# A transformer step of 1072 tokens: chunks of 384, 384 and 304, two long blocks, and a new order at the norms

## The chip, the core and the metric

The kernel runs on one core of a Trainium2 chip (trn2). The metric is the device time of one execution in microseconds; the median of several runs is what counts.

## What is computed

One step of a one-layer encoder for 1072 tokens (16 meta tokens, 1024 of a prompt, 32 of running streams), width 1024, in float32:

```python
def swiglu(x, wg, wu, wd):
    return (jax.nn.silu(x @ wg) * (x @ wu)) @ wd
def ffn_step(h, g, b, wg, wu, wd):
    return layer_norm(ALPHA * h + 0.5 * swiglu(h, wg, wu, wd), g, b)
```

A first such step (hidden width 2816) with norm ln1; then one product with `w_in` that gives the inputs of two mixers, a sparse attention whose keys are picked by an index score, and a recurrence; then `mixer_output`, in which each mixer's output goes through a projection, is weighted by a gate, and the sum through `w_out`, with norm ln2; then a second feed-forward step with norm ln3.

## The kernel before, in words

Activations lie transposed in SBUF: `c.y` holds 128 rows of the width on the partitions, 8 slices of them, by 1072 tokens. Every large product is exact to nearly float32 by splitting both operands into a high and a low part: `product3` (line 63) issues three products (L65 to L67) into one bank of PSUM. ScalarE makes the high parts, GpSimd or VectorE the low ones (the "rests").

Tokens are taken in the chunks of line 31, `[(0, 358), (358, 358), (716, 356)]`; tiles of 128 tokens (`TT`) are used where tokens are turned to or from the partitions.

`build` (line 1849) runs seven phases, each a block of its own that ends with `end_phase` (clear the semaphores, a barrier over all engines):

- `load_inputs` (line 110): SyncE loads tiles of tokens into three buffers, TensorE transposes each (L152), ScalarE makes `h_hi` and `y` (L169, L170), VectorE `h_lo` (L177). The first weights of ffn1 are loaded ahead (L133).
- `ffn` (line 295) for ffn1: 11 groups of 256 hidden rows, of two tiles j. An "up" is one (j, chunk): 48 products for gate and up, then silu on ScalarE (L373), the product and its split on VectorE (L485, L490, L492). Then the "downs": 8 outputs of 6 products per chunk into two banks, which VectorE adds to `y` (L504). The first group is ordered by chunk, all others by tile; all six ups come ahead of the three downs. GpSimd makes the weights' rests (L418, L425).
- `index_and_project` (line 730): first norm ln1 (class `Norm`, line 181). Per chunk: `mean` (L215) and `variance` (L224) are products with a matrix of ones on TensorE, `centre` is on VectorE (L274), `squares` (L240) and `deviation` (L247) on ScalarE, `scale_shift` on VectorE (L281 reciprocal, L287 two multiplications, L291 eight scale-and-shifts, then the rest of the second half, L262); `heads` (L252) makes `h_hi` on ScalarE, the first half's rest is GpSimd's. All three chunks' means and variances are issued together; then tiles 0 and 1 of the projection (class `Projection`, line 654) go chunk by chunk, every later tile by itself. ScalarE drains, `QueryStack` splits the index queries (L637, L643), and the index scores follow (L650, L651).
- `mixers` (line 1139).
- `mixer_output` (line 1682): four pairs of tiles t. Per pair all six ups (24 products each, L65 to L67 into `mo_psa` and `mo_psb`), the gated sum on VectorE (`mix`), then the downs of three chunks into four banks, which VectorE adds to `y` (L1842, L1846). `y` comes back from DRAM during the second tile (L1725).
- `ffn` for ffn2 with ln2 at its head, and `last_norm` (line 514): nine tiles are transposed back (L555), VectorE makes the moments (L592 to L601), ScalarE normalises (L582), GpSimd multiplies by gamma (L566), VectorE adds beta (L611), SyncE stores.

Every engine runs its list of instructions in order and waits on semaphores; the order of each list is written by hand.

Of the kernel before, what the change touches and what calls it, by code (L numbers as in the profile page):

```python
# [7 lines left out]

# [22 lines left out]
CHUNKS = [(0, 358), (358, 358), (716, 356)]  # L31
# [37 lines left out]

class Core:  # L70


# [13 lines left out]
    def sb(self, stack, name, shape, dtype=F32):  # L86
        return stack.enter_context(self.nc.sbuf_tensor(name, shape, dtype))

    def ps(self, stack, name, shape):
        return stack.enter_context(self.nc.psum_tensor(name, shape, F32))  # L90

# [18 lines left out]
def load_inputs(c, dram):  # L110

    nc = c.nc
    with ExitStack() as st:
        x = c.sb(st, "ld_x", [P, 3, D])
        psT = [c.ps(st, f"ld_ps{i}", [P, KD * P]) for i in range(2)]
        x_in = [c.sem(f"ld_x_in{i}") for i in range(3)]
        ident_ready, w_in = c.sem("ld_ident"), c.sem("ld_w")
        turned, hi_done, lo_done, y_done = (c.sem("ld_" + n) for n in ("turned", "hi", "lo", "y"))
        n_dma = [sum(bool(token_rows(t, *r)) for r in ((0, N_META), (N_META, LP), (LP, T))) for t in range(len(TT))]
        with nc.Block() as block:  # L120
            @block.sync
            def _(sp):
                for t in range(len(TT)):
                    if t >= 3:
                        sp.wait_ge(turned, t - 2)
                    for src, r0, r1 in ((dram["meta"], 0, N_META), (dram["x_prompt"], N_META, LP),
                                        (dram["x_sample"], LP, T)):
                        if (rows := token_rows(t, r0, r1)):
                            p0, n, at = rows
                            sp.dma_start(x[p0:p0 + n, t % 3, :], src[at:at + n, :]).then_inc(x_in[t % 3], 16)  # L130
                    if t == 4:
                        for i, part in enumerate(("ffn1_wg", "ffn1_wu")):
                            sp.dma_start(c.up_raw[:, i], dram[part].rearrange("(k p) m -> p k m", p=P)[:, :, 0:2 * P]).then_inc(w_in, 16)  # L133
                sp.wait_ge(w_in, 32)

            @block.gpsimd
            def _(pool):
                pool.memset(c.ident[:], 0.0).then_inc(ident_ready, 1)
                pool.wait_ge(ident_ready, 1)
                pool.affine_select(out=c.ident[:], in_=c.ident[:], compare_op=ALU.not_equal, fill=1.0, base=0,  # L140
                                   pattern=[[-1, P]], channel_multiplier=1).then_inc(ident_ready, 1)

            @block.tensor
            def _(pe):
                pe.wait_ge(ident_ready, 2)
                for t, (t0, n) in enumerate(TT):
                    pe.wait_ge(x_in[t % 3], 16 * sum(n_dma[t % 3:t + 1:3]))
                    if t >= 2:
                        pe.wait_ge(lo_done, t - 1)
                        pe.wait_ge(y_done, t - 1)  # L150
                    for k in range(KD):
                        last = pe.transpose(psT[t % 2][:, k * P:k * P + n], x[0:n, t % 3, k * P:(k + 1) * P],  # L152
                                            c.ident[0:n, 0:n])
                    last.then_inc(turned, 1)

            drain_transposed(c, block, psT, turned, hi_done, lo_done, y_done)


def transposed(ps, n):
    return ps[:].rearrange("p (k t) -> p k t", k=KD)[:, :, 0:n]  # L160


def drain_transposed(c, block, psT, turned, hi_done, lo_done, y_done):

    @block.scalar
    def _(act):
        for t, (t0, n) in enumerate(TT):
            act.wait_ge(turned, t + 1)
# [12 lines left out]
class Norm:
# [4 lines left out]
    def __init__(self, c, st, name, banks, eps, scratch=None):  # L186
        self.c, self.name, self.banks, self.eps_value = c, name, banks, eps
        sb = lambda n, s: c.sb(st, f"{name}_{n}", s)
        self.gamma, self.beta, self.eps, self.ones = sb("gamma", [P, KD]), sb("beta", [P, KD]), sb("eps", [P, 1]), sb("ones", [P, P])
        self.sd, self.rstd = sb("sd", [P, 358]), sb("rstd", [P, 358])  # L190
        self.sq = sb("sq", [P, 2, 2, 358]) if scratch is None else scratch
# [103 lines left out]
def ffn(c, dram, name, norm_name=None):  # L295

    nc = c.nc  # L300
    wg = dram[name + "_wg"].rearrange("(k p) m -> p k m", p=P)
    wu = dram[name + "_wu"].rearrange("(k p) m -> p k m", p=P)
    wd = dram[name + "_wd"].rearrange("(n p) m -> p n m", p=P)
    with ExitStack() as st:
        sb = lambda n, s, d=F32: c.sb(st, f"{name}_{n}", s, d)
        sem = lambda n: c.sem(f"{name}_{n}")

        up_raw = sb("up_raw", [P, 2, KD, 2 * P]) if norm_name else c.up_raw
        loads_ahead = 0 if norm_name else 1
        up_hi = sb("up_hi", [P, 2, 2, KD, P], F32R)  # L310
        up_lo = sb("up_lo", [P, 2, 2, KD, P], F32R)
        dn_raw = sb("dn_raw", [P, 2, D])
        dn_hi = sb("dn_hi", [P, 2, D], F32R)
        dn_lo = sb("dn_lo", [P, 2, D], F32R)
        hid_hi = sb("hid_hi", [P, 2, T], F32R)
        hid_lo = sb("hid_lo", [P, 2, T], F32R)
        gate = sb("gate", [P, 2, 358])
        prod = sb("prod", [P, 2, 358])
        ps_gate = [c.ps(st, f"{name}_psg{i}", [P, 512]) for i in range(3)]
        ps_up = [c.ps(st, f"{name}_psu{i}", [P, 512]) for i in range(3)]  # L320
        ps_dn = [c.ps(st, f"{name}_psd{i}", [P, 512]) for i in range(2)]
        up_in, dn_in = sem("up_in"), sem("dn_in")
        up_hi_done, up_lo_done, dn_hi_done, dn_lo_done = sem("uphi"), sem("uplo"), sem("dnhi"), sem("dnlo")
        up_mm, dn_mm = sem("up_mm"), sem("dn_mm")
# [1598 lines left out]
```

## Time and profile before

| | us |
|---|---|
| runs, median (lowest to highest of 3) | 2971.89 (2968.1 to 2976.58) |
| span of the profiled execution | 2966.0 |
| load to the first feed-forward product | 0 to 40.40 |
| ffn1 | 40.40 to 829.1 |
| ln1, first projection tiles, to the first score | 829.1 to 961 |
| scores, selection, rest of the projection | 961 to 1465 |
| mixers | 1465 to 1880 |
| mixer_output | 1880 to 2082.7 |
| ln2 and ffn2 | 2082.7 to 2921.6 |
| last norm | 2921.6 to 2966 |

The page gives no time of the profiled execution besides its span, the time from its first to its last instruction; the runs contain what lies around it. Engines are named PE (TensorE), PEld (its weight loads), DVE (VectorE), ACT (ScalarE), POOL (GpSimd), SP (SyncE). PEclk is the mean clock that TensorE was granted, 1.00 being 2.4 GHz. A matmul's own duration overlaps that of the next, so starts tell the spacing.

### The profile page before, as it was taken

The numbers are of one execution on the slowest core, as the hardware profiler recorded it, in microseconds if no ns is written. First come the engines' busy times: TensorE is split into PE (matmuls) and PEld (weight loads), VectorE is DVE, ScalarE is ACT, GpSimd is POOL, SyncE is SP. The second block draws the span as 40 slices with busy tenths as digits, with TensorE's granted clock in tenths as the row PEclk, the third lists the DMA queues.
The fourth block names the chain that finished last, engine by engine and source line by source line (L and its number), as shares of the span: only waits on it lengthen the run. The fifth ranks groups of instructions, "written<-read, shape, count | busy, mean of one in ns | idle before, by whom it ended". The sixth has DMA issues, their size and how long they took to land. (4 is left out here: it accounts for less than half of the span.)

```text
span 2966.0 us, 41425 instructions
## 1 busy us (share of the span) xinstructions
PE 2739.8 (92%) x16384; PEld 2638.8 (89%) x16384; DVE 1378.5 (46%) x2882; ACT 632.2 (21%) x1081; POOL 513.7 (17%) x183
## 2 busy tenths in 40 slices
PE   6999999999978999999869986799799999999995
PEld 6999999999957899999759975799599999999995
DVE  1333333333356689993075526666553333333336
ACT  3111111111023622122245533210311111111102
POOL 1211111122012012112100002121221112222112
PEclk9999999999988999999858987799999999999997
DMA  3111111111022011222200000422211111111101
GB/s 130 53 48 42 42 42 42 42 42 42 1 60 63 22 36 43 95 88 95 89 15 31 1 1 8 154 67 73 71 43 43 42 42 42 42 50 49 42 0 73
DMA packets 134941, 149.13 MB, mean 50 GB/s; under 512 B 19072, under 2 KB 119520, under 8 KB 134704
## 3 DMA queue, kind: packets, MB, share of 16 engines
q1 hardware_dynamic: 131376, 134.45, 14.4%
q10 hardware_dynamic: 3456, 13.17, 1.1%
q8 instruction: 75, 1.23, 0.2%
q14 instruction: 34, 0.28, 0.0%
HBM read 123.82 MB, written 23.79 MB: 50 GB/s over the span
## 5 line engine op out<-in xcount | busy, mean ns | idle before, releaser
L485 DVE TENSOR_TENSOR ffn_prod<-ffn_gate,ffn_psu 128x358 f32<-128x358 f32 x132 | 69.6, 527 | 808.3 <-ACT ffn_gate L373 808.3
L65 PE MATMUL ffn_psg<-h_hi,ffn_up_hi 128*128 128x358 f32 (+1 forms) x1056 | 345.4, 327 | 23.8 <-DVE h_lo L262 12.5
L65 PE MATMUL ixp_ps<-h_hi,ixp_hi 128*128 128x358 f32 (+1 forms) x1032 | 338.7, 328 | 24.3 <-issue 17.3
L65 PE MATMUL ffn_psd<-ffn_hid_hi,ffn_dn_hi 128*128 128x358 f32 (+1 forms) x1056 | 346.6, 328 | 11.4 <-DVE y L504 10.4
L504 DVE TENSOR_TENSOR y<-y,ffn_psd 128x358 f32<-128x358 f32 (+1 forms) x480 | 251.0, 526 | 209.4 <-PE ffn_psd L67 209.4
L66 PE MATMUL ffn_psg<-h_lo,ffn_up_hi 128*128 128x358 f32 (+1 forms) x1056 | 346.1, 328 | 0.0
L67 PE MATMUL ffn_psg<-h_hi,ffn_up_lo 128*128 128x358 f32 (+1 forms) x1056 | 345.5, 327 | 0.0
L373 ACT ACTIVATE ffn_gate<-ffn_psg 128x358 f32<-128x358 f32 x132 | 62.0, 470 | 1329.7 <-PE ffn_psu L67 1329.7
L66 PE MATMUL ffn_psd<-ffn_hid_lo,ffn_dn_hi 128*128 128x358 f32 (+1 forms) x1056 | 344.5, 326 | 0.0
L66 PE MATMUL ffn_psu<-h_lo,ffn_up_hi 128*128 128x358 f32 (+1 forms) x1056 | 344.3, 326 | 0.0
L67 PE MATMUL ffn_psd<-ffn_hid_hi,ffn_dn_lo 128*128 128x358 f32 (+1 forms) x1056 | 344.3, 326 | 0.0
L67 PE MATMUL ffn_psu<-h_hi,ffn_up_lo 128*128 128x358 f32 (+1 forms) x1056 | 343.6, 325 | 0.0
L65 PE MATMUL ffn_psu<-h_hi,ffn_up_hi 128*128 128x358 f32 (+1 forms) x1056 | 342.6, 324 | 0.0
L66 PE MATMUL ixp_ps<-h_lo,ixp_hi 128*128 128x358 f32 (+1 forms) x1032 | 338.9, 328 | 0.0
L67 PE MATMUL ixp_ps<-h_hi,ixp_lo 128*128 128x358 f32 (+1 forms) x1032 | 337.6, 327 | 0.0
L425 POOL TENSOR_TENSOR ffn_dn_lo<-ffn_dn_raw,ffn_dn_hi 128x2048 fp32r<-128x2048 f32 x22 | 101.8, 4626 | 892.3 <-ACT ffn_dn_hi L379 892.3
L65 PEld LDWEIGHTS ffn_psg<-h_hi,ffn_up_hi 128*128 128x128 f32 x1056 | 200.0, 189 | 25.1 <-issue 14.8
L65 PEld LDWEIGHTS ffn_psd<-ffn_hid_hi,ffn_dn_hi 128*128 128x128 f32 x1056 | 198.0, 188 | 26.3 <-DVE y L504 16.4
L65 PEld LDWEIGHTS ixp_ps<-h_hi,ixp_hi 128*128 128x128 f32 x1032 | 195.9, 190 | 26.0 <-issue 21.8
L67 PEld LDWEIGHTS ffn_psg<-h_hi,ffn_up_lo 128*128 128x128 f32 x1056 | 200.2, 190 | 0.0
L66 PEld LDWEIGHTS ffn_psg<-h_lo,ffn_up_hi 128*128 128x128 f32 x1056 | 199.9, 189 | 0.0
L66 PEld LDWEIGHTS ffn_psd<-ffn_hid_lo,ffn_dn_hi 128*128 128x128 f32 x1056 | 199.1, 189 | 0.0
(289 smaller groups left out, 4936.2 us busy)
## 6 DMA issues: line engine op xcount, KB each, us to landing
ffn_dn_raw<-in_ffn_wd SPq DMA_DIRECT2D x22, 1024.0 KB, 4.9
ixp_raw<-in_w_in SPq DMA_DIRECT2D x39, 512.0 KB, 3.8
spill<-y ACTq DMA_DIRECT2D x24, 536.0 KB, 2.7
up_raw<-in_ffn_wg SPq DMA_DIRECT2D x11, 1024.0 KB, 5.4
up_raw<-in_ffn_wu SPq DMA_DIRECT2D x11, 1024.0 KB, 7.9
ffn_up_raw<-in_ffn_wg SPq DMA_DIRECT2D x11, 1024.0 KB, 5.4
ffn_up_raw<-in_ffn_wu SPq DMA_DIRECT2D x11, 1024.0 KB, 7.9
mo_sig<-spill SPq DMA_DIRECT2D x16, 536.0 KB, 4.7
```

Of the source, the lines that this page charges most:

```text
L65: pe.matmul(out, w_hi, x_hi, start=first, stop=False)
L66: pe.matmul(out, w_hi, x_lo, start=False, stop=False)
L67: return pe.matmul(out, w_lo, x_hi, start=False, stop=last)
L373: act.activation(gate[:, k % 2, 0:w], ps_gate[k % 3][:, 0:w], ACT.Silu).then_inc(silu_done, 1)
L425: pool.tensor_tensor(dn_lo[:], dn_raw[:], dn_hi[:].bitcast(F32), ALU.subtract).then_inc(dn_lo_done, 1)
L485: dve.tensor_tensor(prod[:, k % 2, 0:w], gate[:, k % 2, 0:w], ps_up[k % 3][:, 0:w], ALU.mult).then_inc(prod_done, 1)
L504: dve.tensor_tensor(y, y, ps_dn[o % 2][:, 0:w], ALU.add).then_inc(y_done, 1)
```

## The change

- `CHUNKS` becomes 384, 384 and 304 tokens: the first two are three whole tiles each.
- Every buffer has a fixed address. Load, ffn1 and ln1 (`front`) share a block with `index_and_project`; `mixer_output`, ln2, ffn2 and ln3 (`back`) share another. Three barriers are left of seven.
- Start: each tile of x has a buffer of its own. SyncE loads tiles 0 to 2, the first weights of j = 0, tiles 3 to 5, those of j = 1, tiles 6 to 8. TensorE turns tiles 0 to 2, then does the first group's ups with tiles 3 to 8 turned between. VectorE makes the first weights' rests.
- Last group of each ffn by chunk, with two banks each for gate and up: up 0, 1, 2, down 0, up 3, down 1, up 4, up 5, down 2; between them stand mean 0, variance 0, mean 1 of ln1 (ffn1) or transposes of the last norm (ffn2).
- VectorE adds the last chunk's down sums, then scales the first chunk; this holds for ln1 and for ln2. The rest of ln1 is in the index block.
- The projection's first four tiles go chunk by chunk (`FIRST = 4`), with four weight buffers.
- `mixer_output`: each pair goes by chunk (up 0, 1, 2, down 0, up 3, 4, down 1, up 5, down 2), the last one with mean 0, variance 0, mean 1 of ln2 between. ln2's gamma and beta and the first weights of ffn2 are loaded behind `y`. The last pair's downs use two banks.
- Last norm: tiles 0 to 2 are normalised ahead of the last sums; the rows are scaled and shifted in place.

The core of the diff:

```diff
-CHUNKS = [(0, 358), (358, 358), (716, 356)]
+CW = 384
+CHUNKS = [(0, 384), (384, 384), (768, 304)]
...
+def front(c, block, dram, st):
...
+    @block.sync
+    def _(sp):
+        for j in range(2):
+            for t in range(3 * j, 3 * j + 3):
+                ld.load(sp, t)
+            f.load_up_first(sp, j)
+        for t in range(6, 9):
+            ld.load(sp, t)
+        f.load_down_first(sp)
+        f.loads(sp)
...
+    @block.tensor
+    def _(pe):
+        for t in range(3):
+            ld.turn(pe, t)
+        for x, j, n in f.BY_CHUNK:
+            if x < 2:
+                pe.wait_ge(f.up_lo_done, j + 1)
+            if j == 0:
+                pe.wait_ge(ld.lo_done, 3 * n + 3)
...
+            f.up_half(pe, x, j, n, 0)
+            if x == 2:
+                ld.turn(pe, 7)
+            f.up_half(pe, x, j, n, 1)
+            if x == 0:
+                for t in range(3, 6):
+                    ld.turn(pe, t)
...
+        f.pe_middle(pe)
+        f.up_last(pe, 0)
+        f.up_last(pe, 1)
+        f.up_last(pe, 2)
+        f.down_last(pe, 0)
+        f.up_last(pe, 3)
+        pe.wait_ge(f.y_done, 24 * L + 8)
+        norm.mean(pe, 0)
+        f.down_last(pe, 1)
+        f.up_last(pe, 4)
+        norm.variance(pe, 0)
+        f.up_last(pe, 5)
+        pe.wait_ge(f.y_done, 24 * L + 16)
+        norm.mean(pe, 1)
+        f.down_last(pe, 2)
...
+    @block.vector
+    def _(dve):
...
+        for k in range(3):
+            f.hidden_last(dve, k)
+        f.sums_last(dve, 0)
+        f.hidden_last(dve, 3)
+        f.sums_last(dve, 1)
+        norm.centre(dve, 0)
+        f.hidden_last(dve, 4)
+        f.hidden_last(dve, 5)
+        f.sums_last(dve, 2)
+        norm.scale_shift(dve, 0)
...
+def index_and_project(c, block, dram, st, f, norm):
...
+    def _(pe):
+        norm.ready(pe, 0)
+        pe.wait_ge(f.prod_done, 6 * GROUPS)
+        pr.multiply(pe, 0, 0)
+        norm.variance(pe, 1)
+        pr.multiply(pe, 1, 0)
+        pe.wait_ge(f.y_done, 24 * GROUPS)
+        norm.mean(pe, 2)
+        pr.multiply(pe, 2, 0)
+        pr.multiply(pe, 3, 0)
+        norm.variance(pe, 2)
+        for i in (1, 2):
+            norm.ready(pe, i)
+            for n in range(pr.FIRST):
+                pr.multiply(pe, n, i)
...
+    def _(dve):
+        norm.centre(dve, 1)
+        norm.centre(dve, 2)
+        norm.scale_shift(dve, 1)
+        norm.scale_shift(dve, 2)
+        for n in range(4):
+            queries.rests(dve, n, iq[:, n, :])
...
+def back(c, block, dram, st):
...
+        for i in range(PAIRS):
+            for x in range(3):
+                up(i, x)
+            down(i, 0)
+            up(i, 3)
+            if i == PAIRS - 1:
+                pe.wait_ge(y_done, 24 * i + 8)
+                norm.mean(pe, 0)
+                up(i, 4)
+                down(i, 1)
+                up(i, 5)
+                norm.variance(pe, 0)
+                pe.wait_ge(y_done, 24 * i + 16)
+                norm.mean(pe, 1)
+            else:
+                up(i, 4)
+                down(i, 1)
+                up(i, 5)
+            down(i, 2)
+        pe.wait_ge(y_done, 24 * PAIRS)
+        norm.mean(pe, 2)
+        for x, j, n in f.BY_CHUNK:
+            if j == 0:
+                norm.ready(pe, n)
...
+            f.up(pe, x, j, n)
+            if x == 0:
+                norm.variance(pe, 1)
+            if x == 1:
+                norm.variance(pe, 2)
...
+    def _(dve):
...
+            sums(i, 2)
+        norm.scale_shift(dve, 0)
+        norm.centre(dve, 1)
+        norm.centre(dve, 2)
+        f.hidden(dve, 0, 0, 0, 0, first=True)
+        norm.scale_shift(dve, 1)
+        f.hidden(dve, 0, 1, 1, 0, first=True)
+        norm.scale_shift(dve, 2)
```

`ready` makes TensorE wait for both halves of a chunk's `h_lo`. In the index block ScalarE makes chunk 2's `heads` only after its drains of tiles 0 to 3 of chunk 1, and splits tile 4's weights after those of chunk 2.

## Rows read from the trace of the kernel before

**Rows 1.** table of stretches: from:to, length, busy us and count of each engine, PEclk, DMA, GB/s
```profile
0.00:40.40 40.40, 15.99 (x72) 13.76 (x72) 10.26 (x9) 22.23 (x22) 5.25 (x8) 1.00 0.56 187
40.40:89.50 49.10, 49.09 (x289) 49.09 (x290) 7.04 (x15) 5.96 (x7) 13.67 (x3) 1.00 0.20 65
89.50:757.30 667.80, 662.59 (x4033) 655.56 (x4033) 223.53 (x404) 76.61 (x83) 128.69 (x28) 1.00 0.13 43
757.30:961.00 203.70, 167.84 (x909) 154.06 (x907) 100.64 (x136) 48.52 (x68) 32.27 (x14) 0.93 0.15 44
1880.00:1939.30 59.30, 49.10 (x289) 48.62 (x290) 41.89 (x59) 14.08 (x12) 14.89 (x6) 0.91 0.53 192
1939.30:2082.70 143.40, 142.07 (x865) 141.18 (x864) 90.15 (x163) 10.62 (x10) 24.35 (x10) 1.00 0.22 72
2082.70:2182.30 99.60, 81.10 (x385) 68.25 (x386) 56.61 (x58) 33.69 (x34) 29.65 (x9) 0.91 0.20 64
2849.90:2966.00 116.10, 83.77 (x506) 80.78 (x504) 55.81 (x97) 19.29 (x26) 25.80 (x11) 0.85 0.13 47
```

**Rows 2.** TensorE's waits, whole run: waiter, releaser: us in total, times, longest
```profile
PE ixp_ps L65 <- issue: 17.3, 2, 12.4
PE ffn_psg L65 <- DVE h_lo L262: 12.5, 1, 12.5
PE ln_psA L555 <- ACT ln_xh L582: 10.1, 5, 2.7
PE ffn_psg L65 <- POOL ffn_up_lo L418: 10.1, 1, 10.1
PE mo_psa L65 <- POOL mo_up_lo L1758: 9.1, 1, 9.1
PE ix_ps L650 <- DVE y L979: 6.9, 1, 6.9
```

**Rows 3.** timeline of TensorE at 980 us: start, duration, instruction
```profile
980.25 0.28 PE L650 MATMUL ix_ps<-k_hi,q_stack 128*128 128x264 f32 x1
980.37 0.28 PE L651 MATMUL ix_ps<-k_lo,q_stack 128*128 128x264 f32 x1
980.49 0.28 PE L650 MATMUL ix_ps<-k_hi,q_stack 128*128 128x264 f32 x1
```

**Rows 4.** DMA issues of the page: count, KB each, median us from issue to landing
```profile
up_raw<-in_ffn_wu SPq DMA_DIRECT2D x11, 1024.0 KB, 7.9
y<-y_spill SPq DMA_DIRECT2D x1, 4288.0 KB, 14.5
```

**Rows 5.** groups of VectorE, GpSimd, ScalarE by shape: busy us, mean ns of one, idle before
```profile
L177 DVE TENSOR_TENSOR h_lo<-ld_ps,h_hi 128x1024 fp32r<-128x1024 f32 x8 | 9.8, 1225 | 22.8 <-ACT y L170 22.8
L418 POOL TENSOR_TENSOR ffn_up_lo<-up_raw,ffn_up_hi 128x2048 fp32r<-128x2048 f32 x22 | 101.1, 4595 | 178.1 <-ACT ffn_up_hi L366 178.1
L566 POOL TENSOR_TENSOR ln_xg<-ln_xh,ln_gamma 128x1024 f32<-128x1024 f32 x8 | 18.8, 2344 | 15.3 <-DVE ln_xn L611 8.0 <-ACT ln_xh L582 7.4
L582 ACT ACTIVATE ln_xh<-ln_psA,ln_nb,ln_rs 128x1024 f32<-128x1024 f32 x8 | 9.6, 1204 | 6.3 <-DVE ln_nb L601 6.3
```

**Rows 6.** groups of TensorE, 829.1 to 961 us, one of them
```profile
L224 PE MATMUL ix_ps<-ix_scratch,ln_ones 128*128 128x358 f32 x32 | 10.1, 467 | 2.1 <-ACT ix_scratch L240 2.1
```

**Rows 7.** timeline of VectorE, the scaling of the first chunk ahead of ffn2
```profile
2101.44 2.39 DVE L281 RECIPROCAL ln_rstd<-ln_sd 128x358 f32<-128x358 f32 x1 [3.85 <-ACT ln_sd L247]
...
2107.04 3.09 DVE L291 TENSOR_SCALAR y<-y,ln_gamma,ln_beta 128x358 f32<-128x358 f32 x8
2111.60 3.30 DVE L262 TENSOR_TENSOR h_lo<-y,h_hi 128x1432 fp32r<-128x1432 f32 x1 [1.46 <-ACT h_hi L252]
```

**Rows 8.** timeline of GpSimd at the start of mixer_output
```profile
1893.82 2.64 POOL L1758 TENSOR_TENSOR mo_up_lo<-mo_up_raw,mo_up_hi 128x1024 fp32r<-128x1024 f32 x1 [5.81 <-ACT mo_up_hi L1733]
1903.86 2.46 POOL L1763 TENSOR_TENSOR mo_dn_lo<-mo_dn_raw,mo_dn_hi 128x1024 fp32r<-128x1024 f32 x1 [4.76 <-ACT mo_dn_hi L1739]
```

**Rows 9.** groups of TensorE's weight loads, whole run, one of them
```profile
L65 PEld LDWEIGHTS ffn_psg<-h_hi,ffn_up_hi 128*128 128x128 f32 x1056 | 200.0, 189 | 25.1 <-issue 14.8 <-POOL ffn_up_lo L418 10.2
```

More of the change, by code:

```diff
@@ L9 @@
+import math
 from contextlib import ExitStack
@@ L107, in store_rows @@
     return 48
[L110 to L156, printed above, removed]
@@ L666, in __init__ @@
             c.sem(f"{name}_{n}") for n in ("hi_done", "lo_done", "mm", "drained"))
[L668 removed]
+        F = self.FIRST
+        order = [(n, i) for i in range(3) for n in range(F)] + [(n, i) for n in range(F, len(tiles)) for i in range(3)]
         self.at = {x: k for k, x in enumerate(order)}
@@ new lines, in index_and_project @@
+    pr = Projection(c, "ixp", dram["w_in"], tiles, banks[0:4])
+    ps_s, ps_misc = banks[4:7], banks[7]
+    low = Region(c, 139328, c.DN_RAW)
+    scratch, dist = low.take("ix_scratch", [P, 2 * LP]), low.take("ix_dist", [P, LP])
+    relu = scratch[:, 0:3 * 512].rearrange("p (n k) -> p n k", n=3)
+    run = scratch[:, 0:LP]
+    eq = scratch[:, LP:2 * LP].bitcast(BF16).rearrange("p (n k) -> p n k", n=2)
+    high = Region(c, 204224, c.NORM + 9728)
+    ks_t = high.take("ix_ks_t", [P, NS])
+    ks_hi, ks_lo = high.take("ix_ks_hi", [P, NS], F32R), high.take("ix_ks_lo", [P, NS], F32R)
@@ new lines, in index_and_project, with scores @@
+    h_out = [sem(f"h_out{i}") for i in range(3)]
+    units = []
+    for b in list(range(1, NB)) + ["s"]:
+        for h in range(HEADS):
+            units += [(b, h, k0, w) for k0, w in pieces(SCORE_AT[b][1])]
+    EARLY = 9
+    gap = len(units) // EARLY
+    early = {gap * (j + 1) - 1: (NI + j // 3, j % 3) for j in range(EARLY)}
+    index = {x[:3]: n for n, x in enumerate(units)}
+    blocks = [(n, b, QB) for n, b in enumerate(range(1, NB))] + [(NB - 1, "s", DEC)]
+    def scores(b, rows):
+        at, keys = SCORE_AT[b]
+        return c.score[0:rows, at:at + keys]
@@ new lines, in _ @@
+    @block.sync
+    def _(sp):
+        norm.load(sp, dram)
+        sp.wait_ge(f.up_lo_done, 2 * GROUPS)
+        pr.load(sp, 0)
+        pr.load(sp, 1)
+        for half in range(2):
+            sp.dma_start(kidx_rows[:, :, half * DH:(half + 1) * DH],
+                         dram["cache_kidx"].rearrange("(n p) d -> p n d", p=P)).then_inc(kidx_in, 16)
+        pr.load(sp, 2)
+        pr.load(sp, 3)
+        for n in range(3):
+            t0, w = CHUNKS[n]
+            sp.wait_ge(norm.shifted, KD * (n + 1))
+            sp.dma_start(c.y_spill[:, :, t0:t0 + w], c.y[:, :, t0:t0 + w]).then_inc(h_out[n], 16)
+        for n in range(4, NI + 3):
+            pr.load(sp, n)
+        sp.wait_ge(ki_done, len(TT))
+        n_out = store_rows(sp, ki_tok, dram["new_kidx_p"], dram["new_kidx_s"], ki_out)
+        for n in range(NI + 3, NTL):
+            pr.load(sp, n)
+        sp.wait_ge(ki_out, n_out)
@@ new lines, in back @@
+    dn_hi, dn_lo = at(177920, "dn_hi", [P, 2, KD, P], F32R), at(177920 + 8192, "dn_lo", [P, 2, KD, P], F32R)
+    sig = [[at(o, f"sig{t}{g}", [P, T]) for g, o in enumerate(os)]
+           for t, os in enumerate(((c.UP_HI, c.UP_HI + 4288), (c.UP_HI + 8576, c.DN_HI + 12288)))]
+    pa, pb = at(c.GATE, "pa", [P, CW]), at(c.GATE + 1536, "pb", [P, CW])
+    with ExitStack() as own:
+        ps = [[c.ps(own, f"mo_ps{n}{i}", [P, 512]) for i in range(2)] for n in "ab"]
+        ps_dn = [c.ps(own, f"mo_psd{i}", [P, 512]) for i in range(4)]
@@ new lines, in back @@
+    up_in, dn_in, sig_in = (sem(n) for n in ("up_in", "dn_in", "sig_in"))
+    y_in = sem("y_in")
+    x_hi_done, x_lo_done, up_hi_done, up_lo_done, dn_hi_done, dn_lo_done = (
+        sem(n) for n in ("xhi", "xlo", "uphi", "uplo", "dnhi", "dnlo"))
+    up_mm, mul_done, sum_done, mhi_done, mix_done, dn_mm, y_done = (
+        sem(n) for n in ("up_mm", "mul", "sum", "mhi", "mix", "dn_mm", "y"))
+    ln = LastNorm(c, dram, "ln3")
+    f = ln.f = Ffn(c, st, dram, "ffn2")
+    norm = Norm(c, "ln2", f.ps_dn, LN_EPS)
```

1787 lines of the change are left out of this document (958 added, 829 removed).

## Prediction

> **What bounds the kernel now.** I read the table by stretches first [rows 1]. In the long feed-forward stretch (89.50 to 757.30 us) TensorE is busy 662.59 of 667.80 us at full clock, 4033 products in all, 0.1656 us for a product of about 358 columns; the pairs of mixer_output (1939.30 to 2082.70) are as dense. These stretches can only gain through the cost of a product. What can be won lies at the seams: 40.40 us before the first feed-forward product; 203.70 us from the last group of ffn1 to the first index score, with TensorE busy 167.84 and a mean clock of 0.93; 99.60 us from mixer_output's last product to the first down products of ffn2 (busy 81.10, clock 0.91); and 116.10 us for the last group of ffn2 with the last norm (busy 83.77). The table of waits names what ends them [rows 2]: a VectorE h_lo (12.5 us in one wait), two waits without a named releaser (17.3), GpSimd's weight rests at both starts (10.1 and 9.1), the y chain ahead of the scores (6.9), and ScalarE's ln_xh in the last norm (10.1).
>
> A seam also costs clock: 203.70 us at 0.93 and 99.60 us at 0.91 mean that TensorE went to its lower level of 1.2 GHz after the waits [rows 1].
>
> **Chunk widths: zero.** Each product is run at 384, 384 and 304 columns where it was 358, 358 and 356; the sum is 1072 either way. Is a product linear in its columns? Products of 264 columns start 0.12 us apart, one behind the other [rows 3]; 0.1656 us times 264/358 is 0.122. So 384 costs 0.178 and 304 costs 0.141, and three together stay at 0.497. Bounds from the same rows: 1 ns per triple either way over 4,584 triples (22 groups of 144, 43 projection tiles of 24, four pairs of 96), 5 us.
>
> **Start: 13 us won.** The change drops the barrier between load and ffn1, gives every x tile its own buffer, queues x tiles 0 to 2 and the first half of the weights ahead, and lets products begin after three tiles. Two 1 MB loads issued together land within 7.9 us [rows 4], about 0.24 MB per us with the second issue's half microsecond; 2.5 MB so take 10.4 us, and land near 12. ScalarE meanwhile makes six copies of about 1 us each (22 instructions in 22.23 us in the first stretch [rows 1]), then the split, to about 15. The rest of the first weights moves from GpSimd (4595 ns) to VectorE [rows 5]: not seen there, so 2.45 us by its nearest row, 1225 ns for 1024 elements, and at most 4.6 at GpSimd's price. I take 2.45, since GpSimd is idle then. The first product starts near 17.5 where it was at 40.40. The Trainium skill (VectorE: DVE Perf Modes, the perf-mode tier table) gives 2293 ns for such a float32 operation of 2048 elements; by it the gain would be 0.2 us larger, and no run here shows it yet.
>
> From there the six ups last 49.10 us as before, but six tiles are still transposed between them. 72 transposes took 15.99 us [rows 1], 0.22 each; 48 cost 10.7 at that price and 5.3 if the clock is doubled by then; I take 7.5. One transpose waits for ScalarE's copies of tile 3, which stand behind the first silu: 2.5 us. Group 0's downs start at 17.5 + 49.1 + 7.5 + 2.5 = 76.6 instead of 89.5. Ends: 8 to 17 us.
>
> **From ffn1 to the scores: 7 us lost.** The work: six ups and three downs of the last group 71.5 us (432 products at 0.1656), five projection tiles 59.6 (360 products), six means and variances at about 5 us each (32 products of a variance in 10.1 us [rows 6]) 29.9, small transposes 2; 163 us in all. Before, 41 us of 203.70 were thus wait and low clock. The new order, chunk by chunk with two banks, puts a mean, a variance and a mean among the ups and downs, where VectorE and ScalarE are ahead; that part should not stall, and the barrier (some 1.6 us) goes. But VectorE adds the last chunk's sums and only then scales chunk 0, and the projection waits for that. The chain stands in the trace [rows 7]: reciprocal, two multiplications, eight scale-and-shifts, the h_hi copy, the rest: 2101.44 to 2114.90, 13.5 us, and 14.4 at 384 columns. With 0.7 for the last sum TensorE waits 15 us, and I take 2.4 for the low clock that follows. After that centre 2 must wait for mean 2, and scale 1 stands behind it on VectorE: TensorE has four products of chunk 0, a variance and a mean to cover it, and runs dry for about 5 us before chunk 1. The h_hi copy of chunk 2 is put behind ScalarE's drains of all four tiles of chunk 1: 5.5 us before chunk 2. Tile 4's weights reuse tile 0's buffer and are split only after those drains: 4 us. Last, the index's query splits of four tiles, which before were done one pair at a time, now come in a clump after chunk 2, so the scores start about 10.5 us after tile 4 and its transposes instead of 6.9. With 6 for the low clock after these three shorter waits, and 1 for small ones, the loss is 0.7 + 15 + 2.4 + 5 + 5.5 + 4 + 10.5 + 6 = 49, less about 1 that overlaps; 48 against 41. Ends: 15 us lost where every wait also costs its full clock, 3 won if the shorter waits are covered.
>
> **mixer_output and ffn2's start: 8 us lost.** Each pair is now done by chunk. In pair 0, three ups (12.7 us) stand ahead of the first downs instead of six (23.6). Three things come late. The second tile's up rests are ready at 1896.46 (GpSimd starts them at 1893.82 [rows 8]), TensorE's first up ends near 1894: 2.6 us. The second down rest ends at 1906.3 [rows 8]: 0.6 to 1.5 us. And the sums of the first chunk need y, which has 4288 KB and takes 14.5 us [rows 4]; it is issued behind the second down weights and sig, near 1900.5, 4 us sooner than before, so it lands near 1915.5, while the four PSUM banks are full at 1910.7: 5 us. With 2 for the low clock, pair 0 takes about 60 us where it took 51.2 (the 59.30 of [rows 1] less 8.1 ahead of its first product): 9 lost. At the other end the first ffn2 weights are ready, and a mean, variance and mean go among the last pair, 15.6 us of work that was serial; but again VectorE scales chunk 0 after the last sums (14.4 us, of which mean 2 covers 4.1): 10.5 us wait and 2.4 of clock. Then centre 1 and 2, hidden 0 and scale 1 stand in one queue on VectorE, and hidden 0 waits for ScalarE's squares of chunk 1, which wait for TensorE's variance: I get 6.5 us before chunk 1, 2 for the clock. Together some 22 us of wait against 99.60 - 47.2 - 29.9 = 22.5 before. So the far end is even, and the start's 9 us are the loss, less the barrier that is inside: 8. Ends: 15 lost, none lost.
>
> **Last norm: 4.5 us won.** Each tile costs GpSimd 2.34 us in series with ScalarE's 1.2 [rows 5]. Three of nine tiles move ahead: 10.7 won, and the barrier's 1.8. Against it stand five tiles' transposes among the products (4.4), 1.5 of stall, and 2 because tile 2 waits for the last sums on VectorE. Ends: 0 to 8.
>
> The mixers between are not changed but for addresses: zero, bounded by 2 us either way, the spread of dense stretches.
>
> **Sum:** 13 - 7 - 8 + 4.5 = 2.5 us won on a span of 2966.0. The span is 5.9 below the median of the runs, 2971.89; against that median the forecast is 2969.4, rounded to 2969. No change is what lies within 0.3%, 9 us: 2963 to 2981.
>
> **The rivals.**
> *The seams break even or better.* Before chunk 1 and 2 the cover is short by only 5 us each; if ScalarE's table loads or VectorE's contention with GpSimd are less than in [rows 7], the two inner seams lose nothing at all, and the chunked order then keeps all of 13 + 4.5: 2954, and with the upper ends 17 + 3 + 8 it is 2944. For it speaks that the chain's rest is measured beside GpSimd (3.30 us for 1432 elements, against 1225 ns for 1024 alone [rows 5, 7]); against it, that the wait behind the last sums is certain.
>
> *The scale behind the last sums costs clock for long.* The 0.93 and 0.91 in [rows 1] show that waits at these seams bring 1.2 GHz with them, and by the steps above the new order has eight waits of 4 us or more there where the old had about five. At the lower ends, 15 and 15 lost, the sum is 13 + 4.5 - 30: 12.5 slower, 2984. It decides from the point where both seams together lose 26.5 us, 11 more than forecast.
>
> *A narrow product isn't cheaper.* A weight load shows as 189 ns [rows 9]; if 304 columns cost 0.164 us like 356, 25 ns times 4,584 triples are 115 us: 3084. From 6.5 ns per triple on the kernel is slower by 0.3%. The 264-column starts at 0.12 us speak against it. The Trainium skill (TensorE: Matmul & The Clock Gate, Back-to-back issue gap) says that in a stream of weight loads and products both set the spacing; the trace agrees only as far as that load stays under 0.12 us.
>
> *The overlap doesn't come about*, because the first x tiles and weights share the DMA engines with all that is queued behind: the start gains only 8, and the sum is 2.5 slower, inside no change.
>
> **How the numbers follow.** The forecast's case, no change, with the last rival: 0.37. Seams even or better: 0.41, all faster. Clock and waits: 0.16, slower. Narrow products: 0.06, slower. The range leaves out the narrow products and the outer parts of the second and third case: 2945 to 2986. The likeliest case alone spans 2963 to 2981.
>
> **What would show it.** Right: the first feed-forward product before 21 us and group 0's downs before 82; a wait of about 15 us on h_lo in the seam after ffn1, and one of 10 after mixer_output; a wait of 5 us on y in pair 0; products of 304 columns 0.14 us apart. Wrong: waits on h_lo under 5 us, dense stretches longer than 667 us, or a first product after 25 us.

## The result, and the profile after

The changed kernel takes 2979.91 us in the median (2976.52 to 2982.39, 5 runs), against 2971.89 (2967.32 to 2976.58) before: 8 us more, or 0.27% by the medians. The ratio of the runs is put at 1.0034, with a 95% interval of 1.0021 to 1.0048: slower by a little, and clear of noise. The profiled execution has a span of 2979.3 us, 13.3 more than the 2966.0 of before. The forecast was 2969, in a range of 2945 to 2986: 2.5 us faster, which counts as no change. That case had a chance of 0.37, a faster kernel 0.41 and a slower one 0.22; the sign is the less likely one.

The stages, cut in both traces at the same TensorE instructions (start of the first product that the stage names):

| stage | before | after | measured | forecast |
|---|---|---|---|---|
| start to group 0's downs of ffn1 | 89.5 | 73.2 | 16.3 won | 13 won |
| ffn1, groups 0 to 10 | 667.9 | 665.4 | 2.5 won | 0 |
| last group of ffn1 to the first score | 203.7 | 210.3 | 6.6 lost | 7 lost |
| scores, projection, mixers | 927.0 | 926.0 | 1.0 won | 0 |
| mixer_output and ln2, to group 0's downs of ffn2 | 294.2 | 328.1 | 33.9 lost | 8 lost |
| ffn2, groups 0 to 10 | 667.7 | 665.4 | 2.3 won | 0 |
| last group of ffn2, last norm | 116.1 | 110.8 | 5.2 won | 4.5 won |

One row carries the miss: 25.9 us more than forecast, while the six others together are 10 us better. The table of stretches after, with the columns of [rows 1]:

```profile
0.00:17.40 17.40, 4.47 (x24) 4.06 (x24) 5.97 (x4) 8.68 (x8) 0.71 (x6) 0.85 0.94 289
17.40:73.20 55.80, 54.55 (x336) 53.92 (x337) 16.05 (x22) 19.45 (x21) 8.74 (x2) 0.96 0.32 102
73.20:738.70 665.50, 662.93 (x4035) 655.98 (x4034) 218.23 (x404) 76.83 (x83) 129.49 (x29) 1.00 0.14 44
738.70:948.90 210.20, 169.36 (x908) 156.23 (x908) 94.97 (x136) 50.82 (x70) 33.79 (x14) 0.89 0.12 36
...
1875.00:1944.80 69.80, 56.32 (x289) 54.81 (x289) 38.22 (x57) 7.73 (x8) 13.36 (x5) 0.85 0.50 165
1944.80:2055.00 110.20, 97.83 (x579) 96.11 (x578) 60.73 (x108) 8.48 (x8) 19.44 (x8) 0.97 0.24 79
...
2868.40:2979.30 110.90, 82.53 (x506) 79.73 (x504) 52.86 (x97) 24.55 (x30) 25.79 (x10) 0.87 0.11 40
```

The first two stretches and the last gain as forecast. Look at the sixth, pairs 1 and 2 of mixer_output: 110.20 us, with TensorE busy 97.83. The same two pairs before are one dense block:

```profile
1939.30:2035.40 96.10, 94.83 (x578) 94.23 (x578) 61.23 (x108) 8.49 (x8) 19.18 (x8) 1.00 0.28 90
```

Idle time went from 1.27 to 12.37 us, and the clock from 1.00 to 0.97. The table of TensorE's waits after names what ends it (columns as in [rows 2]; line numbers are those of the new kernel; the rows of the mixers and some others are left out):

```profile
PE ixp_ps L67 <- issue: 20.6, 2, 14.7
PE mo_psd L67 <- DVE mo_mix_lo L2143: 16.9, 4, 4.8
PE mo_psa L67 <- POOL mo_up_lo L2005: 10.3, 2, 8.5
PE ffn_psg L67 <- issue: 9.8, 1, 9.8
...
PE ffn_psg L67 <- DVE h_lo L281: 7.1, 1, 7.1
...
PE ixp_ps L1037 <- DVE ix_ks_t L1146: 6.6, 1, 6.6
...
PE ixp_ps L67 <- DVE h_lo L281: 5.2, 1, 5.2
...
PE mo_psd L67 <- DVE y L2155: 4.1, 2, 3.3
PE ixp_ps L67 <- POOL ixp_lo L859: 3.9, 1, 3.9
PE ix_ps L808 <- DVE y L1164: 3.7, 1, 3.7
```

The second row is new: four waits on `mo_mix_lo`, 16.9 us, one of 3.2 us in pair 0's first downs and one of 4.4 to 4.8 us in the third downs of each of pairs 0, 1 and 2. Here is the one of pair 1, in the timeline of the new kernel, first VectorE, then TensorE and GpSimd:

```profile
1987.25 0.47 DVE L2132 TENSOR_TENSOR mo_pa<-mo_sig,mo_psa 128x304 f32<-128x304 f32 x1 [3.22 <-PE mo_psb L69]
1987.64 0.46 DVE L2132 TENSOR_TENSOR mo_pb<-mo_sig,mo_psb 128x304 f32<-128x304 f32 x1
1988.14 2.52 DVE L2135 TENSOR_TENSOR mo_pa<-mo_pa,mo_pb 128x304 f32<-128x304 f32 x1
1990.70 0.32 DVE L2141 CAST mo_mix_hi<-mo_pa 128x304 fp32r<-128x304 f32 x1
1991.05 0.47 DVE L2143 TENSOR_TENSOR mo_mix_lo<-mo_pa,mo_mix_hi 128x304 fp32r<-128x304 f32 x1
...
1986.46 0.30 PE L69 MATMUL mo_psb<-mo_x_hi,mo_up_lo 128*128 128x304 f32 x1
1991.58 0.43 PE L67 MATMUL mo_psd<-mo_mix_hi,mo_dn_hi 128*128 128x304 f32 x1 [4.82 <-DVE mo_mix_lo L2143]
1991.82 0.44 PE L68 MATMUL mo_psd<-mo_mix_lo,mo_dn_hi 128*128 128x304 f32 x1
...
1987.99 2.34 POOL L2005 TENSOR_TENSOR mo_up_lo<-mo_up_raw,mo_up_hi 128x1024 fp32r<-128x1024 f32 x1 [10.21 <-ACT mo_up_hi L1941]
```

TensorE issues the last product of up 5 at 1986.46, and next in its list stand downs 2, which need the mix of just that up. The five VectorE operations of the mix stand between, and nothing of TensorE's does. One of them, the add of L2135, takes 2.52 us, and ends 0.33 us after GpSimd's rest. In pairs 0 and 2 the add begins 0.2 us ahead of that rest and takes 0.47 us; there the cast behind it takes 2.34 us. Behind the wait products of 304 columns start 0.24 us apart, at a granted clock of 0.50 (1991.9 to 1995.1 us), where in the dense stretches it is 0.14 (shown below).

### The profile page after: what moved, and what is told of

Same layout as the page of the kernel before. It is cut to its first block and busy times, and to the rows that moved or that the text cites. A ratio compares the mean times of both kernels' runs of the same rounds, so it can differ in the third digit from the quotient of the medians.

```text
span 2979.3 us, 41370 instructions
## 1 busy us (share of the span) xinstructions
PE 2747.3 (92%) x16384; PEld 2646.9 (89%) x16384; DVE 1360.9 (46%) x2884; ACT 641.8 (22%) x1089; POOL 507.5 (17%) x181
## 5 line engine op out<-in xcount | busy, mean ns | idle before, releaser
L67 PE MATMUL ffn_psg<-h_hi,ffn_up_hi 128*128 128x384 f32 (+1 forms) x1056 | 348.0, 330 | 23.5 <-issue 9.8
L67 PE MATMUL ixp_ps<-h_hi,ixp_hi 128*128 128x384 f32 (+1 forms) x1032 | 340.6, 330 | 29.7 <-issue 20.6
L67 PE MATMUL ffn_psd<-ffn_hid_hi,ffn_dn_hi 128*128 128x384 f32 (+1 forms) x1056 | 353.3, 335 | 8.0 <-DVE y L503 6.2
L68 PE MATMUL ffn_psg<-h_lo,ffn_up_hi 128*128 128x384 f32 (+1 forms) x1056 | 345.4, 327 | 0.0
L69 PE MATMUL ffn_psg<-h_hi,ffn_up_lo 128*128 128x384 f32 (+1 forms) x1056 | 344.6, 326 | 0.0
L67 PE MATMUL ffn_psu<-h_hi,ffn_up_hi 128*128 128x384 f32 (+1 forms) x1056 | 344.0, 326 | 0.0
L69 PE MATMUL ffn_psd<-ffn_hid_hi,ffn_dn_lo 128*128 128x384 f32 (+1 forms) x1056 | 343.3, 325 | 0.0
L68 PE MATMUL ffn_psd<-ffn_hid_lo,ffn_dn_hi 128*128 128x384 f32 (+1 forms) x1056 | 343.2, 325 | 0.0
L69 PE MATMUL ffn_psu<-h_hi,ffn_up_lo 128*128 128x384 f32 (+1 forms) x1056 | 343.0, 325 | 0.0
L68 PE MATMUL ffn_psu<-h_lo,ffn_up_hi 128*128 128x384 f32 (+1 forms) x1056 | 342.1, 324 | 0.0
## 6 DMA issues: line engine op xcount, KB each, us to landing
y<-y_spill SPq DMA_DIRECT2D x1, 4288.0 KB, 16.5
```

Of the source, the lines that this page charges most:

```text
L67: pe.matmul(out, w_hi, x_hi, start=first, stop=False)
L68: pe.matmul(out, w_hi, x_lo, start=False, stop=False)
L69: return pe.matmul(out, w_lo, x_hi, start=False, stop=last)
```

## Experiments

Two theories stood after this. By one, the new order of the pairs (downs 2 straight behind up 5) makes the loss, in every pair but the last. By the other, it lies in the loads of pair 0 and in the operation that is stretched beside GpSimd's rest. Besides, the seams' long waits had been attributed to the scale behind the last sums, and the dense stretches' gain to the widths. Each was tried alone. One stretch that no experiment reorders, from the first score to mixer_output, takes between 920.0 and 927.0 us in the ten kernels of this document, so an edit is judged by the stretch that it changes, and the whole time comes second.

**Widths alone.** The kernel before, with the widths and the buffers that hold a chunk:

```diff
-CHUNKS = [(0, 358), (358, 358), (716, 356)]
+CHUNKS = [(0, 384), (384, 384), (768, 304)]
...
-        self.sd, self.rstd = sb("sd", [P, 358]), sb("rstd", [P, 358])
+        self.sd, self.rstd = sb("sd", [P, 384]), sb("rstd", [P, 384])
```

> The kernel before with the chunks 384, 384, 304 and nothing else of the change. Theory: products are linear in their columns, so the widths cost nothing; the dense stretch of ffn1 from group 0's downs to the last group's first up takes 665 to 668 us (before 667.9), the whole 2962 to 2974. Rival: the loss of 8 us comes from the narrow chunk; then this kernel stands at 2978 or more.

Measured: 2961.23 us, ratio to before 0.9960 (0.9945 to 0.9975); span 2959.1, 6.9 less than before. The two dense stretches take 665.3 and 665.2 us, as in the changed kernel (665.4 both), so what was gained there is the widths' alone. The time lies just under the 2962 to 2974 that were expected. A product of 304 columns is thus not paid like one of 358: in the timeline of the changed kernel such products start 0.14 us apart, and those of 384 columns 0.17.

```profile
400.61 0.30 PE L69 MATMUL ffn_psg<-h_hi,ffn_up_lo 128*128 128x304 f32 x1
400.75 0.30 PE L67 MATMUL ffn_psg<-h_hi,ffn_up_hi 128*128 128x304 f32 x1
...
410.29 0.34 PE L69 MATMUL ffn_psu<-h_hi,ffn_up_lo 128*128 128x384 f32 x1
410.46 0.34 PE L67 MATMUL ffn_psu<-h_hi,ffn_up_hi 128*128 128x384 f32 x1
```

It follows that the rest of the change, the two long blocks and the orders, costs about 20 us of span (6.9 + 13.3); it is by no means neutral.

**Order of the pairs.** In the changed kernel, up 5 ahead of downs 1, and on VectorE mix 5 ahead of sums 1, for pairs 0 to 2:

```diff
                 up(i, 4)
-                down(i, 1)
                 up(i, 5)
+                down(i, 1)
             down(i, 2)
```

> The changed kernel, but in pairs 0 to 2 of mixer_output the last up stands ahead of the second downs, and VectorE mixes it ahead of the second sums. Theory: TensorE's wait of 4.7 to 5.1 us on the last mix of each of these pairs, with 1.4 to 2 us of low clock behind it, is what the forecast missed; then pairs 1 and 2 take 48 us instead of 55, pair 0 is 6 shorter, and the whole stands near 2960 (2956 to 2964). Rival: the wait only moves to the downs of chunk 1 or to their sums in two more banks; then under 6 us are won, 2974 or more.

Measured: 2953.44 us, ratio 0.9931 (0.9911 to 0.9951); span 2951.1, 28.2 less than after. The pairs take 61.13, 47.53 and 48.13 us where they took 69.84, 55.06 and 55.13, and the wait in front of the third downs is gone. Pairs 0 and 1 in the table of stretches:

```profile
1870.20:1931.30 61.10, 52.11 (x288) 51.09 (x289) 36.64 (x57) 7.70 (x8) 12.30 (x5) 0.92 0.59 193
1931.30:1978.80 47.50, 46.96 (x290) 46.59 (x289) 28.31 (x54) 4.25 (x4) 9.68 (x4) 1.00 0.28 91
```

Pair 1 is dense again (46.96 busy of 47.50) and at full clock. The order makes 8.7 + 7.5 + 7.0 = 23.2 us. The other 5 lie in stretches that the edit does not touch (2.7 in the middle, from score to mixer_output, and about 1 each at the start and in the first seam), and with them the time falls below the 2956 that were expected at least. An operation beside GpSimd is still stretched here, but independent products now cover it. In VectorE's and GpSimd's timelines of this run, in pair 0:

```profile
1914.23 0.47 DVE L2135 TENSOR_TENSOR mo_pa<-mo_pa,mo_pb 128x304 f32<-128x304 f32 x1
1914.74 2.39 DVE L2141 CAST mo_mix_hi<-mo_pa 128x304 fp32r<-128x304 f32 x1
...
1914.44 2.51 POOL L2005 TENSOR_TENSOR mo_up_lo<-mo_up_raw,mo_up_hi 128x1024 fp32r<-128x1024 f32 x1 [25.96 <-ACT mo_up_hi L1941]
```

The add, which began 0.21 us ahead of GpSimd's rest, takes its 0.47; the cast, which began behind it, takes 2.39 instead of 0.32 and ends 0.18 after it.

**GpSimd's rest behind the mix.** In the changed kernel, each pair's second up rest waits until the mixes of the pair are done:

```diff
             if t + 2 < KD:
                 rest_up(t + 2)
+                pool.wait_ge(mix_done, 3 * t + 6)
                 rest_up(t + 3)
```

> The changed kernel, but GpSimd makes the second up rest of the next pair only after the last mix of this one. Theory: the add of the last mix takes 2.5 us because it runs beside GpSimd, 0.5 alone; so TensorE's wait ahead of the third downs falls from 4.8 to 2.8 us, a pair from 55.1 to 53, the whole by 6. Rival one: the wait is the chain itself, and nothing changes. Rival two: with 2.8 us the clock stays up, and a pair falls to 51.

Measured: 2971.29 us (one run); pairs 66.18, 53.38 and 52.42 us. The add in its timeline, and pair 1 in the table of stretches:

```profile
1983.06 0.47 DVE L2136 TENSOR_TENSOR mo_pa<-mo_pa,mo_pb 128x304 f32<-128x304 f32 x1
```

```profile
1939.30:1992.70 53.40, 49.06 (x290) 48.20 (x289) 28.32 (x54) 4.25 (x4) 9.70 (x4) 0.97 0.24 81
```

The add takes 0.47 us when GpSimd does nothing beside it, so 2.05 of its 2.52 us were GpSimd's. The wait ahead of the third downs falls by 2.0 us in each of the three pairs, also where it was the cast that was stretched. In pairs 1 and 2 that is worth 1.7 and 2.7 us of some 7; the rest is the mix itself, 2.8 and 2.4 us of wait, and the clock (0.97 still). The Trainium skill (SBUF — State Buffer, section SBUF: two separate sides) says that VectorE and GpSimd share one pair of ports, which goes to one instruction for its whole length while the other engine's blocks, and counts a VectorE operation with two inputs in SBUF among those that need it. The trace agrees: the add that began 0.15 us behind GpSimd's rest ended only after it, and in the run with the other order the add that began 0.21 ahead of it did not wait.

**Loads of pair 0.** In the changed kernel, `y` comes back by chunks with a semaphore each, the first one ahead of the second down weights, and the second `sig` as soon as the inputs are split:

```diff
+            if t == 1:
+                t0, w = CHUNKS[0]
+                sp.dma_start(c.y[:, :, t0:t0 + w], c.y_spill[:, :, t0:t0 + w]).then_inc(y_in[0], 16)
+                sp.wait_ge(x_lo_done, 6)
+                for g, spilled in enumerate((SP_GA, SP_GB)):
+                    sp.dma_start(sig[1][g][:], c.spill[spilled + 1]).then_inc(sig_in[1], 16)
...
-                sp.dma_start(c.y[:], c.y_spill).then_inc(y_in, 16)
+                for n, (t0, w) in list(enumerate(CHUNKS))[1:]:
+                    sp.dma_start(c.y[:, :, t0:t0 + w], c.y_spill[:, :, t0:t0 + w]).then_inc(y_in[n], 16)
```

> The changed kernel, but y comes back by chunk, its first chunk ahead of the second down weights, and the gates of the second tile as soon as their place is free. Theory: pair 0 waits for the gates (1.9 us more than for the down rests) and 3.6 us for y, with the clock that costs; it takes 63 to 65 us instead of 69.8, the whole 5 to 7 less. Rival: the second down weights now land later behind y's first chunk and take the place of that wait; then pair 0 is not shorter by more than 2.

Measured: 2970.07 us (one run); pair 0 takes 61.73 us instead of 69.84, pairs 1 and 2 stay at 55.01 and 54.53. What it took away is read in VectorE's and TensorE's timelines of the changed kernel:

```profile
1892.20 0.56 DVE L2132 TENSOR_TENSOR mo_pa<-mo_sig,mo_psa 128x384 f32<-128x384 f32 x1 [5.62 <-DMA mo_sig<-spill]
1894.95 0.41 PE L67 MATMUL mo_psd<-mo_mix_hi,mo_dn_hi 128*128 128x384 f32 x1 [3.17 <-DVE mo_mix_lo L2143]
...
1903.62 0.56 DVE L2155 SCALAR_TENSOR_TENSOR y<-y,mo_psd 128x384 f32<-128x384 f32 x1 [6.14 <-DMA y<-y_spill]
1904.23 0.69 PE L67 MATMUL mo_psd<-mo_mix_hi,mo_dn_hi 128*128 128x384 f32 x1 [3.27 <-DVE y L2155]
```

VectorE waits twice for a load, for `sig` and for `y`, and each time TensorE waits 3.2 to 3.3 us behind it. With the new loads the second wait is gone, and of the first 1.75 us are left, now on GpSimd's rest of the second down weights:

```profile
1892.16 0.44 PE L67 MATMUL mo_psd<-mo_mix_hi,mo_dn_hi 128*128 128x384 f32 x1 [1.75 <-POOL mo_dn_lo L2019]
```

So 4.7 of the 8.1 us are waits (1.4 and 3.3), and with them pair 0's mean granted clock rises from 0.85 to 0.92. The 8.1 us are a little more than the 5 to 7 that were expected. The loads are thus about half of pair 0's loss, and no part of that of pairs 1 and 2.

**Scale ahead of the last sums.** In the changed kernel, VectorE scales chunk 0 of ln1 first:

```diff
-        f.sums_last(dve, 2)
         norm.scale_shift(dve, 0)
+        f.sums_last(dve, 2)
```

> The changed kernel, but at the end of ffn1 VectorE scales chunk 0 ahead of the last chunk's down sums. Theory: the chain of 14.2 us is the same, and TensorE now stands inside the last downs with two full banks instead of behind them; the seam from the last group of ffn1 to the first score takes 207 to 211 us against 210.3, the whole 2976 to 2981. Rival: that order is what costs the 15 us; then the seam is 10 us or more shorter, 2970.

Measured: 2971.31 us (one run); the stretch from the last group of ffn1 to the first score takes 206.6 us instead of 210.3 (209.3 to 210.7 in the four other runs that leave this seam as it is). The whole fell below the 2976 to 2981 that were expected, but 4.7 us of that lie in the middle, which the edit does not touch. The wait does not go: it moves ahead of the last downs, which have two banks and need the sums to free them. TensorE's largest wait of that stretch:

```profile
PE ffn_psd L67 <- DVE y L503: 12.0, 2, 11.5
```

One wait of 11.5 us stands where one of 14.7 stood. So the named step, adding the last sums and then scaling, costs 3 to 4 us in this seam against its opposite; the bulk of the wait is the scale itself, wherever it stands.

**Order and loads together.** Both edits of above:

> The pair order of the second run and the loads of the fourth together. Theory: they end different waits of pair 0, so it takes 53 to 56 us (61.1 and 61.7 with one of them), pairs 1 and 2 48; the whole 2944 to 2949. Rival: both shorten pair 0 by the same wait; then it stays at 60, 2952.

Measured: 2945.49 us, ratio 0.992 (0.9893 to 0.9947). Pair 0 takes 52.78 us: 17.1 less than after, where the two edits alone gave 8.7 and 8.1, so they add up. Pair 0 is then within 2.3 us of the kernel with the widths alone (50.50), and pairs 0 to 2 together within 1.6 (147.77 against 146.22).

The new order by chunk without these two faults wins: the span is 20.0 us shorter than with the widths alone. The start wins 16.5, the last norm 4.6 and the far end 2.6, the first seam loses 7.8 and the pairs 1.6; the other 6.0 are the middle's.

**The next chunk ahead of the scale.** On top of the last kernel, at both seams: centre 1 ahead of scale 0 on VectorE, variance 1 ahead of TensorE's wait for chunk 0, squares and deviation 1 ahead of head 0 on ScalarE, and scale 1 straight behind scale 0. For the first seam (the far end of mixer_output likewise):

```diff
         f.sums_last(dve, 2)
+        norm.centre(dve, 1)
         norm.scale_shift(dve, 0)
...
+        norm.variance(pe, 1)
         norm.ready(pe, 0)
         pe.wait_ge(f.prod_done, 6 * GROUPS)
         pr.multiply(pe, 0, 0)
-        norm.variance(pe, 1)
```

> As the run before, and at both seams VectorE centres chunk 1 ahead of scaling chunk 0, TensorE takes chunk 1's variance while it waits for that scaling, and chunk 1 is scaled straight behind chunk 0. Theory: the wait ahead of chunk 0 cannot go (it grows by centre 1's 3.4 us) but now holds the variance's 4.9, and the waits of 5.7 and 7.5 us ahead of chunk 1 with their clock go: the first seam 8 to 11 us shorter, the second 9 to 12, the whole near 2927 (2922 to 2934). Rival: chunk 1 is ready no sooner, because ScalarE's copies and squares bind, and each seam gains less than 3.

Measured: 2930.22 us, ratio 0.9866 (0.9833 to 0.99). The first seam falls from 209.8 to 202.3 us, and the stretch from mixer_output's last down to ffn2's first from 81.9 to 71.7: 7.5 us, just under the 8 expected, and 10.2. TensorE's timeline of the first seam:

```profile
828.47 7.12 PE L243 MATMUL ffn_psu<-ln_sq,ln_ones 128*128 128x384 f32 x16 [3.89 <-DVE y L293]
...
842.80 0.66 PE L67 MATMUL ixp_ps<-h_hi,ixp_hi 128*128 128x384 f32 x1 [7.22 <-issue]
...
871.01 0.41 PE L67 MATMUL ixp_ps<-h_hi,ixp_hi 128*128 128x384 f32 x1 [1.08 <-ACT y L879]
...
893.83 0.59 PE L67 MATMUL ixp_ps<-h_hi,ixp_hi 128*128 128x304 f32 x1 [5.84 <-issue]
```

The variance now lies inside the wait for chunk 0 (3.89 + 7.22 idle instead of 14.75), and the 5.2 us ahead of chunk 1 have become 1.08. The 5.84 us ahead of chunk 2 are untouched.

**The head of chunk 2.** On top of that, ScalarE makes head 2 after two of chunk 1's four drains, not after all:

```diff
-            if i == 2:
-                norm.heads(act, 2)
             act.wait_ge(h_out[i], 16)
             for n in range(4):
+                if i == 1 and n == 2:
+                    norm.heads(act, 2)
```

> As the run before, and in the index block ScalarE copies chunk 2's h_hi after two drains of chunk 1 instead of four. Theory: the wait of 6.2 us ahead of chunk 2 goes with 2 us of clock: the whole 5 to 8 less than the run before. Rival: VectorE's scaling of chunk 2 ends last there, and under 2 are won.

Measured: 2923.59 us, ratio 0.9843 (0.9814 to 0.9872); the first seam falls by another 6.7, to 195.6 us. TensorE's largest waits in it:

```profile
PE ixp_ps L1038 <- DVE ix_ks_t L1146: 7.4, 1, 7.4
PE ixp_ps L67 <- issue: 7.2, 1, 7.2
```

The wait ahead of chunk 2 is gone. This is the fastest of all: 44.8 us (1.5%) below the median of before that ran beside it (2968.38), and 1.2% below the widths alone by the two ratios.

## Why the prediction was right in most parts and wrong in its sum

**Start: right, 16.3 won instead of 13.** The first product came at 17.41 us; the text says 17.5. The rest of the first weights on VectorE took 2.29 us where the text took 2.45, as the Trainium skill (VectorE: DVE Perf Modes, the perf-mode tier table) has it for such an operation:

```profile
15.06 2.29 DVE L403 TENSOR_TENSOR ffn_up_lo<-ffn_up_raw,ffn_up_hi 128x2048 fp32r<-128x2048 f32 x1 [0.49 <-ACT ffn_up_hi L375]
```

Then the ups and transposes took 55.80 us, and not 59.1: TensorE was busy 54.55 of them, at a mean granted clock of 0.96. The 7.5 and 2.5 for transposes and their stall were too much.

**Widths: zero forecast, 6.9 of span won.** The term was nothing, with bounds of 1 ns per triple either way; measured are 2.5 us over 4033 products in ffn1, 0.62 ns a product or 1.9 ns a triple. The rival that a narrow product isn't cheaper is refuted.

**First seam: right, wait by wait.** 6.6 lost against 7. The waits behind the sum have their counterparts in the table of waits: 15 forecast for the scale and 14.7 measured, 5 and 5.2 ahead of chunk 1, 5.5 and 5.9 (20.6 less 14.7) ahead of chunk 2, 4 and 3.9 for tile 4's rests, 10.5 and 6.6 + 3.7 ahead of the scores. For the low clock it had 8.4, an estimate that it works out from no row; TensorE's busy time there, 169.4 us, is 6.4 more than the 163 of work that it counts. The scaling chain is the one of [rows 7], at 384 columns (VectorE, GpSimd, TensorE):

```profile
825.86 2.54 DVE L300 RECIPROCAL ln_rstd<-ln_sd 128x384 f32<-128x384 f32 x1
...
836.53 3.54 DVE L281 TENSOR_TENSOR h_lo<-y,h_hi 128x1536 fp32r<-128x1536 f32 x1 [1.55 <-ACT h_hi L271]
...
835.02 3.44 POOL L281 TENSOR_TENSOR h_lo<-y,h_hi 128x1536 fp32r<-128x1536 f32 x1 [15.09 <-ACT h_hi L271]
...
840.18 0.66 PE L67 MATMUL ixp_ps<-h_hi,ixp_hi 128*128 128x384 f32 x1 [14.75 <-issue]
840.64 0.52 PE L68 MATMUL ixp_ps<-h_lo,ixp_hi 128*128 128x384 f32 x1
840.96 0.52 PE L69 MATMUL ixp_ps<-h_hi,ixp_lo 128*128 128x384 f32 x1
```

From 825.86 to 840.07 it is 14.2 us; the text has 14.4. What was said of the clock shows in the last two rows: products of 384 columns, elsewhere 0.17 us apart, start 0.32 us apart behind the wait; the granted clock there (840.20 to 843.60 us) is 0.50, the level of 1.2 GHz. Overlooked was that the chain's last step, too, is stretched: VectorE's rest of the second half takes 3.54 us beside GpSimd's rest of the first, and ends 1.6 us after it, where each of the two multiplications of that width takes 1.7. By the same sign as in the pairs, some 1.8 us of this wait would be GpSimd's; no run tried it.

**mixer_output: the failed step.** The prediction says "Three things come late" in pair 0 and prices these alone, 9 us. These three were near (the up rests' waits came to 1.8 us beyond the first tile's 8.5, where 2.6 was said; the second down rest to 1.75 in the run with the new loads, where 0.6 to 1.5 was said; `y` to 3.3, where 5 was said). `sig`, which came after that down rest and made the wait 3.2, was left out. What it did not do was to go through the new list of a pair in the steady state: up 5, then downs 2. In the old order a mix had other ups and downs behind it; in the new one nothing stands between up 5 and the downs that need its mix, in three of four pairs. Each costs about 7 us: 4.4 to 4.8 of wait, of which GpSimd makes 2, and the low clock behind it. The widths' run takes 146.2 us for pairs 0 to 2, the changed kernel 180.0: of these 33.8, the order is 23.2 and the loads of pair 0 are 8.1, each by its own run, and both together 32.3; about 1.5 are left. So the step that failed is the term that the prediction put at nothing without a reason: pairs 1 and 2, and the end of pair 0, which it had found "as dense" in the old order and did not look at again in the new one.

**Far end: even, as forecast.** The last pair and ln2 take 148.1 us, 146.9 before; the waits on chunk 0 and 1 of 10.5 and 6.5 were measured as 9.8 and 7.1 (the two rows on `ffn_psg` in the table of waits).

**Last norm: right in its sum,** 5.2 won instead of 4.5; the terms were not read one by one.

**The rivals.** The one that came nearest, clock and waits at the seams (2984), had the right sign and the wrong place: the two seams together behaved as in the forecast, and the loss lay between them. That the time still lies within 2945 to 2986 is luck: the range had no such loss in it, and 10 us of unforeseen gains in the other stretches made up for part of it. That the seams could do better than even is shown by the last two experiments: with chunk 1's centre and variance inside the wait and an earlier head, the first seam takes 195.6 us, 8.1 less than before the change.

Some working of the prediction does not come out as written; none of it makes the miss. Pair 0's terms add up to 10.2 to 11.1 us, not 9. In the first seam the 0.7 for the last sum is counted twice, and the 1 for small waits is named and not added. A narrow product as dear as one of 356 columns would cost 23 ns per triple, not 25, and the kernel is slower by 0.3% from 2.5 ns per triple on, not 6.5. And no change is called the likeliest case, while the faster one has the higher chance.

Not tried: why three products of 384, 384 and 304 columns take 2 ns less than three of 358, 358 and 356; the 7.4 us on `ix_ks_t` ahead of the scores, tile 4's rests, GpSimd's part in the scale and the 7.2 us that are left of chunk 0's wait; whether a later stretch of the middle (920.0 to 927.0 us from kernel to kernel, with no edit in it) can be steered.

## What to carry to other kernels

When an order is made finer, write out one steady turn of the loop for each engine and mark, for every product, what has to happen between its input's last product and itself; where nothing of its own engine lies between, the whole chain of the other engine is paid, once per turn, with the clock behind it. One exchange in the lists of TensorE and VectorE (independent work put between) was worth 23 us here, more than the 16 of the new start. And where a wait for a long chain can't be removed, as for the scale of a norm's first chunk, put the next chunk's small steps into it: exchanging the two kinds of VectorE work, scale and sums, mostly moved the wait and won 3 to 4 us of it.

## What the runs showed of the hardware that was not expected

An add of 304 columns with both inputs in SBUF takes 0.47 us alone and 2.52 us beside a 2.34 us GpSimd instruction. A cast of 304 columns, with one input, takes 2.34 to 2.39 us in that place and 0.32 alone. It could have been read in the kernel before, where the add of 358 columns takes 2.63 us beside GpSimd's rest and that of 356 without it 0.53, hidden behind other products:

```profile
1947.74 2.39 POOL L1763 TENSOR_TENSOR mo_dn_lo<-mo_dn_raw,mo_dn_hi 128x1024 fp32r<-128x1024 f32 x1 [4.67 <-ACT mo_dn_hi L1739]
...
1947.89 2.63 DVE L1816 TENSOR_TENSOR mo_pa<-mo_pa,mo_pb 128x358 f32<-128x358 f32 x1
1952.55 0.53 DVE L1816 TENSOR_TENSOR mo_pa<-mo_pa,mo_pb 128x356 f32<-128x356 f32 x1
```

There the stretched operation cost nothing (the pair is dense); it did once the new order put it on the path. That three products of unequal widths are cheaper by 2 ns than three of equal ones, 5 us over the two dense stretches, was not expected either, and its cause is open.
